# The low parts of the U blocks, in the transition and the last stage, on VectorE in place of GpSimd

## The reference

```python
def one(x):                                     # x: tokens after RMSNorm
    q = (x @ wq).reshape(C, PEER_HEADS, 2, PEER_HALF)
    s = jnp.einsum('chpk,hpnk->chpn', q, sub_keys)
    top_s, top_i = lax.top_k(s, K)              # 16 of 128, twice per head
    cand = top_s[:, :, 0, :, None] + top_s[:, :, 1, None, :]
    best_s, best_j = lax.top_k(cand.reshape(C, PEER_HEADS, K * K), K)
    ...                                         # e = i1 * N_KEYS + i2
    g = jax.nn.softmax(best_s, axis=-1)
    u = jnp.take(expert_u, e, axis=0)
    h = jax.nn.gelu(jnp.einsum('cd,chkd->chk', x, u))
    v = jnp.take(expert_v, e, axis=0)
    return jnp.einsum('chk,chkd->cd', g * h, v)
```

## Time and profile before

| | us |
|---|---|
| median of 3 runs | 3570.25 |
| the runs | 3570.25, 4163.93, 3565.03 |
| the profiled execution | 3574.14 |
| its span, first to last instruction | 3572.3 |
| TensorE busy | 3347.4 |
| VectorE busy | 2547.1 |
| ScalarE busy | 1246.7 |
| GpSimd busy | 1161.9 |

### The profile page before, as it was taken

One profiled execution on the slowest core, in us unless ns is written; L12 is line 12 of the kernel. 1 busy time (PEld: TensorE's weight loads), 2 busy tenths in 40 slices (PEclk: granted clock), 3 DMA queues, 4 the chain that ended last, 5 costly groups with the idle time before them and its releaser, 6 DMA issues.

```text
span 3572.3 us, 55663 instructions
## 1 busy us (share of the span) xinstructions
PE 3347.4 (94%) x17714; PEld 2967.7 (83%) x17714; DVE 2547.1 (71%) x4795; ACT 1246.7 (35%) x2013; POOL 1161.9 (33%) x647
## 2 busy tenths in 40 slices
PE   7999998699879999999999999986998799999999
PEld 6787798699868888888877878886998688888888
DVE  4544699888688676676645547998886877676676
ACT  4433332233333333333344423222332333333332
POOL 3444344101233333333144443441112333333331
PEclk9999999899989999999999999998999899999999
DMA  3111343477788888888521123435677888888885
GB/s 120 65 53 65 107 132 110 165 260 269 283 304 318 310 302 307 304 297 304 202 101 65 53 77 110 126 115 178 247 273 282 303 319 306 309 300 303 298 305 205
DMA packets 235870, 763.87 MB, mean 214 GB/s; under 512 B 19056, under 2 KB 117488, under 8 KB 200688
## 3 DMA queue, kind: packets, MB, share of 16 engines
q1 hardware_dynamic: 198896, 494.09, 39.7%
q0 software_dynamic: 36864, 268.45, 21.8%
HBM read 684.87 MB, written 77.59 MB: 213 GB/s over the span
## 4 chain that ended last, share of the span: by engine, by line
PE 67%; DVE 15%; DVEq 6%; issue 6%; DMA 3%; ACT 1%; POOL 1%; SPq 0%; ACTq 0%; POOLq 0%
PE PS L417 19%; PE PS L419 19%; PE PS L418 19%; PE PS L691 6%; DVE EQ L1268 2%; PE PS L584 1%; DVEq L1277 1%; DVEq L1315 1%; DVE I L1221 1%; DVE I L1228 1%; DMA VRAW<-in_peer_v 1%; DVE SW L1222 1%; POOL RL L1418 1%; PE PS L578 1%; DVE EQ L1272 1%
## 5 line engine op out<-in xcount | busy, mean ns | idle before, releaser
L1418 POOL TENSOR_TENSOR RL<-RAW,RH 128x1024 fp32r<-128x1024 f32 x320 | 801.8, 2515 | 824.2 <-ACT RH L763 823.9
L417 PE MATMUL PS<-XH,RH 128*128 128x384 f32 (+1 forms) x2720 | 985.5, 362 | 21.6 <-ACT GEL L950 21.6
L419 PE MATMUL PS<-XH,RL 128*128 128x384 f32 (+1 forms) x2720 | 957.8, 352 | 0.0
L418 PE MATMUL PS<-XL,RH 128*128 128x384 f32 (+1 forms) x2720 | 956.5, 352 | 0.0
L1452 POOL DMA_INDIRECT ROWS<-in_peer_rows,LIST x256 | 292.0, 1141 | 1449.2 <-DVE X L1316 1405.2
L417 PE MATMUL PS<-VHI,WHI 128*128 128x512 f32 x1536 | 601.9, 392 | 40.9 <-DVE WLO L1375 40.9
L419 PE MATMUL PS<-VHI,WLO 128*128 128x512 f32 x1536 | 600.1, 391 | 0.0
L418 PE MATMUL PS<-VLO,WHI 128*128 128x512 f32 x1536 | 600.1, 391 | 0.0
L1372 DVE TENSOR_TENSOR VLO<-VRAW,VHI 128x1024 fp32r<-128x1024 f32 x256 | 321.6, 1256 | 340.2 <-ACT VHI L958 340.2
L417 PEld LDWEIGHTS PS<-XH,RH 128*128 128x128 f32 x2720 | 520.8, 191 | 50.9 <-issue 22.9
L418 PEld LDWEIGHTS PS<-XL,RH 128*128 128x128 f32 x2720 | 518.6, 191 | 28.3
(11 more groups left out here) (228 smaller groups left out, 3454.3 us busy)
## 6 DMA issues: line engine op xcount, KB each, us to landing
RAW<-in_peer_u SPq DMA_DIRECT2D x256, 512.0 KB, 5.6
VRAW<-in_peer_v SPq DMA_DIRECT2D x256, 512.0 KB, 5.6
RAW<-in_stream SPq DMA_DIRECT2D x128, 512.0 KB, 3.3
route_dram<-STAGE SPq DMA_DIRECT2D x16, 3072.0 KB, 10.1
GC<-route_dram SPq DMA_DIRECT2D x64, 768.0 KB, 8.7
gelu_dram<-GS SPq DMA_DIRECT2D x128, 192.0 KB, 3.6
GB<-gelu_dram SPq DMA_DIRECT2D x32, 768.0 KB, 10.0
ROWS<-in_peer_rows,LIST POOLq DMA_INDIRECT x256, 6.9
```

The lines of the kernel that those rows point to most:

```text
L417: pe.matmul(acc, sh, mh, start=first, stop=False)
L418: pe.matmul(acc, sh, ml, start=False, stop=False)
L419: return pe.matmul(acc, sl, mh, start=False, stop=last)
L1418: pool.tensor_tensor(RL[:, k % 4, :], RAW[:, k % 2, :], RH[:, k % 4, :].bitcast(F32), ALU.subtract).then_inc(S.low_part, 1)
```

## The change

Two VectorE functions are added, `low_of` and `low_at`, which call the `low` that the routing stage has. In the transition VectorE makes the low parts of U blocks 64 and 65 after slots 24 and 25, of 66 and 67 after slot 26, and of 68 and 69 ahead of the last stage. In the last stage it makes one after positions 0, 1, 4 and 5, between `WLO` and `add_row`. GpSimd loses all of these and its wait, and only starts gathers; at the end of a layer it waits until all low parts are made. SP's, ScalarE's and TensorE's lists are the same.

```diff
@@ transition, VectorE
                     dot(k + 1, (k + 1) % RING, (k + 1) // RING)
                     dve.drain()
+                    if k - S_ROUTE < 2:
+                        low_of(J_U + FIRST + 34 + k - S_ROUTE)
+                    elif k - S_ROUTE == 2:
+                        low_of(J_U + FILLED + 2)
+                        low_of(J_U + FILLED + 3)
+                low_of(J_U + FILLED + 4)
+                low_of(J_U + FILLED + 5)
@@ last stage, VectorE
+                def low_at(it, q, ahead):
+
+                    if q in (4, 5) and ahead >= 1:
+                        low(it, J_U + FILLED + q + 2)
+                    if q in (0, 1) and ahead >= 1:
+                        low(it, J_U + FILLED + q + 4)
...
                 for q in range(8):
                     position(0, q)
+                    if q in (4, 5):
+                        low_at(0, q, 2)
...
-                def positions(it, last=False):
+                def positions(it, ahead, last=False):
                     for q in range(8):
                         position(it, q)
+                        low_at(it, q, ahead)
                         if q in AT_Q:
...
-                    positions(it)
-                positions(15, last=True)
+                    positions(it, 2)
+                positions(15, 0, last=True)
@@ GpSimd
-                pool.wait_ge(S.low_part, count(l, "low_part", J_U + FIRST + 34))
                 for k in range(S_TURN):
-                    if k < 2:
-                        low_of(J_U + FIRST + 34 + k)
-                    elif k < 4:
-                        low_of(J_U + FILLED + k)
                     gather(S_ROUTE + k + RING)
-                low_of(J_U + FILLED + 4)
-                low_of(J_U + FILLED + 5)
...
-                        if q == 3 and it < 15:
-                            low_of(J_U + FILLED + 4 * it + 6)
-                            low_of(J_U + FILLED + 4 * it + 7)
-                    if it < 14:
-                        low_of(J_U + FILLED + 4 * it + 8)
-                        low_of(J_U + FILLED + 4 * it + 9)
+                pool.wait_ge(S.low_part, count(l, "low_part", JOBS))
```

More of the change, by code:

```diff
@@ L1323, in low, with low_of @@
                                       ALU.subtract).then_inc(S.low_part, 1)
+                def low_of(n):
+                    low(0, n)
                 dot(0, 0, 0)
```

## The result

| | us |
|---|---|
| before, median of 5 runs | 3570.53 |
| changed, median of 5 runs | 3648.85 |
| ratio, with 95% interval | 1.0209 [1.0192, 1.0226] |
| changed once more, with the first experiments | 3651.71, ratio 1.0229 [1.0209, 1.025] |

The change makes the kernel 2.1% slower, some 75 us. The forecast was 3694 in a range from 3620 to 3800. In each set of five one execution was far slower (4163.93 before, and 8038.62 changed, the profiled one, with TensorE at a mean granted clock of 0.48); the ratio leaves both out, and the rows here are from the second measurement (span 3648.3 us).

The account below looks back on a forecast made before the run. TensorE alone bounds the steady turns at 24.65 us per half turn; a loop of 20.3 + 6.65 = 26.95 us adds 2.3, 124 us in two layers, so 3574.1 + 124 - 4 = 3694 us, range 3620 to 3800.

Parts of the forecast that it names:

- What bounds the kernel: Steady turns of the last stage: TensorE alone sets the time, 669.6 of 670 us busy, 24.65 us per half turn.
- The load on VectorE: Last stage: 4.6 us of added work per turn is hidden by VectorE's 14.6 us idle per 49.3 us turn.
- SP's list: Last stage: the second U block waits for VectorE's low part, holding up V blocks of positions 2, 3, 6, 7.
- The sum 20.3 + L: Half turn loop through VectorE, SP, V transfer and ScalarE: 20.3 us plus the V transfer, 26.95 against TensorE's 24.65.
- L: Time until the V block behind a U block has landed: taken as 6.65 us, bounds 3.1 and 10.6.
- my main case: Last stage: V transfer behind a U block takes 5.7 to 8.5 us, giving 3640 to 3800 us; chance 0.72.
- the rival case: Last stage: V transfer about 5.6 us or less but over 4.35, giving 3570 to 3640 us; chance 0.14.
- The start: Start of the last stage: stretched weighting of 5.64 us becomes 0.57; gain counted as 2 us per layer.
- Counting half turns: Last stages: 27 half turns per layer, each charged 2.3 us, 62 us per layer and 124 in two.
- The clock: Last stage: new TensorE gaps of about 2 us may bring some lower clock, 1 to 2 us per half turn, costing nothing.

Follow-up runs that it names:

- the first experiments: The changed kernel run once more, unaltered, for an undisturbed trace: 3651.71 us, ratio 1.0229.
- SP's list alone: The changed kernel with SP starting each U block behind the V blocks of positions 2, 3, 6, 7: 3559.78 us, ratio 0.9968 to before.
- the place alone: The changed kernel with the last stage's low parts on VectorE in pairs at GpSimd's old places, after positions 3 and 7: 3572.87 us, ratio 1.0008.
- one half freed: The changed kernel with only the U blocks behind position 5 moved behind the V blocks of positions 6 and 7: 3577.38 us, ratio 1.0022.
- the low part 2.6 us later: The changed kernel with each last-stage low part behind its position's add_row and dot instead of ahead of them: 3820.07 us, ratio 1.0696.
- GpSimd late: The kernel before, low parts on GpSimd, with the second of each pair made behind a later gather: 3870.08 us, ratio 1.083.
- the load ahead was 32 KB: The changed kernel with the last stage's hidden U blocks loaded 64 columns wide instead of 1024, waits unchanged: 3568.8 us, ratio 0.9989.

## Why the prediction was right

- **What bounds the kernel.** Right: in the steady turns only TensorE, and the change could lose its full use, not gain. Every variant that came back to TensorE's pace in both halves has half turns of 24.65 us.
- **The load on VectorE.** Right that it is hidden. The WF that reads GB is back at 559 ns, as the one that reads GEL; the 1030 of the earlier trace rows is gone. VectorE does 128 more subtractions in 51 us more of busy time.
- **SP's list.** Right, and shown by SP's list alone (3652 to 3560 us), by the place alone (3573), and by the same loss made with GpSimd.
- **The sum 20.3 + L.** Mean half turn 26.13 and mean L 5.67 leave 20.46. Of its terms, 1309.74 to the end of the second low part was to be 10.1 and was 9.96.
- **L, the term that was mis-sized.** I took 6.65, the middle between the V block's median 5.6 and the U block's 7.7; it was 5.67, which makes 1.48 us instead of 2.3 per half turn, 80 us instead of 124. That is nearly all of the gap between 3694 and 3649, and with it TensorE's busy share in the window is 96% and not 92, a turn 52.3 us and not 54. The 7.7 was no bound for this place. It was the median of U blocks that went out right behind table loads (9.2 and 8.1 us in the mean for the pair behind two tables, 7.1 and 5.7 for the pair behind one). In the changed kernel they go out one by one and some us later behind the tables, and the median is 3.9, as the transfers of its window show:

```profile
VRAW<-in_peer_v SPq DMA_DIRECT2D x104, 512.0 KB, 5.7
RAW<-in_peer_u SPq DMA_DIRECT2D x49, 512.0 KB, 3.9
```

Here the number owes something to the width of the range. The 5.67 lies just under the 5.7 at which my main case began, and the rival case with its 3637 us at L = 5.6, which I gave a chance of 0.14, was nearer to 3649 than the 3694 that I said. I gave it a low chance because nothing said that a block behind another is faster than one by itself. It isn't: in the changed kernel the V blocks of positions 0 and 4, started 7.4 us behind the load before, take 3.3 us in the mean. But the 5.6 of before was itself not the time of a block by itself; it was a median over V blocks that went out among U pairs, tables and gathers. The trace of before also had the V blocks that SP starts right behind the U pair: 3.7 us in the mean of 12 behind one table and the pair, 6.1 behind two tables and the pair. They started 3.3 us after the second U block, not 0.7 us as after the change, and would have given a narrower range than 3.1 to 10.6.
- **The start.** The stretch of 5.64 us went as forecast. But the VHI of turn 1's position 0 is at 1049.86, against 1049.78 before: the low parts and the later V block of turn 0 took back what the start had gained. In the second layer the way from the first VHI to that of turn 1 is 53.9 us, against 57.5 before, but half a turn later both are at 79.4, so there the gain is gone one half turn later. 4 us were counted; by the steady turns none is left. With SP's list mended the same VHI is at 1044.35, and this is where that version gains on the kernel before, twice.
- **Counting half turns.** 54 half turns of one price fitted the change, where all are blocked. As a rule it is wrong: with one half freed, 74 of 92 us came back, not half.
- **The clock.** Gaps of about 2 us might bring some of the lower clock. The 24 gaps of the window are 1.2 us in the mean. Behind one, of 1.91 us, the products took 0.63 us, at a granted clock of 0.55 (1361 to 1364); behind the other 23, up to 2.14 us long, the first product took 0.49 us and the next 0.40 or less, and the window's granted clock is 1.00:

```profile
1334.18 0.49 PE L417 MATMUL PS<-VHI,WHI 128*128 128x512 f32 x1 [0.95 <-DVE WLO L1385]
...
1361.04 0.58 PE L417 MATMUL PS<-VHI,WHI 128*128 128x512 f32 x1 [1.91 <-DVE WLO L1385]
1361.42 0.63 PE L418 MATMUL PS<-VLO,WHI 128*128 128x512 f32 x1
```

Where the gaps are longer, more of it comes: at 3.3 us in the mean (the low part 2.6 us later) the same window has a granted clock of 0.97, at 3.4 us (GpSimd late) 0.94.

## What to carry to other kernels

When work moves to another engine, look for who else waits for its end, and what stands behind that waiter in an in-order list: here a load that waits for a freed buffer held up loads that had nothing to do with it. Cost the loop that this closes (engine, queue, transfer, engine) against the bound's period; it may have been some us shorter and so cost nothing until then. Interleaving the loads by the time at which their buffers come free, rather than in pairs, gave all of it back, and the fastest version of all (3560 us).

## What the runs showed of the hardware

The time of a 512 KB load depended on what was started close to it. In the changed kernel, at a mean DMA share of 0.82 from 1110 to 1760, it was 3.3 us in the mean where SP had started nothing for some 7 us, and 5.67 with 512 KB started 0.7 us ahead and a V block behind. It was 3.6 us where the load ahead was 32 KB, at a share of 0.77. The one transfer that took 10.6 us stood behind tables and two blocks, and the share from 1077 to 1088 was 1.04. The median of the U blocks went from 7.7 to 3.9 us in the changed kernel, but where they start later yet (the low part 2.6 us later) it was 5.5; a later start is not by itself a shorter transfer.

A VectorE weighting that met GpSimd's subtractions took one of three times before. There were two subtractions in a row each time. Where its record began 0.13 us ahead of the first one (28 times) it took 0.56 us, as if alone. Where it began 0.14 us behind (26 times) it took 2.68 and ended 0.4 us after the first subtraction. In each layer's first turn it began while GpSimd was still starting a gather, and there it waited for both subtractions, 5.64 and 5.75 us (4 times):

```profile
993.38 1.62 POOL L1452 DMA_INDIRECT ROWS<-in_peer_rows,LIST  x1 [1.91 <-DVE X L1316]
```

The Trainium skill, "SBUF — State Buffer", section "SBUF: two separate sides", says that of the two engines' instructions the one that starts first gets the shared port pair for the whole instruction. The first two cases agree with it; that a waiting VectorE operation stays behind a second subtraction too, as in the third, it does not say, and no run here shows why.
